# Float32 operands on a 64-byte grid in SBUF: a hybrid decoder step with its dense input halves and gathered expert tokens moved

## The reference

```python
# layer 0: gated DeltaNet mixer, dense SwiGLU; layer 1: short gated convolution, experts
proj = x @ w_in                      # 1024 -> 4112 columns, then conv, silu, delta rule, gate
y = o @ w_out
h = layer_norm(ALPHA * h + y)
h = layer_norm(ALPHA * h + (silu(h @ w_g) * (h @ w_u)) @ w_down)          # d_ff 2816
proj = h @ sc_w_in                   # 1024 -> 3072, gate, 3-tap conv, gate, @ sc_w_out
...
logits = h @ w_router; top_v, top_i = top_k(logits, 2); gates = softmax(top_v)
for e in range(8):                   # d_ff 3584
    y = y + swiglu(h, w_gu[e], w_down[e]) * combine[..., e:e + 1]
h = layer_norm(ALPHA * h + y)
```

## The kernel before

| tile | row pitch, bytes | begins at | rows begin (mod 64) |
|---|---|---|---|
| `raw`, `low` | 8192 | 16512 (0) | 0 |
| `high` | 8192 | 73856 (0) | 0, and 0 for each 128 columns |
| `xres` | 1056 | 108000 (32) | 32, 0, 32, 0, ... |
| `xhb` | 1064 | 116448 (32) | 32, 8, 48, 24, 0, 40, 16, 56 |
| `xlb` | 1064 | 124960 (32) | 32, 8, 48, 24, 0, 40, 16, 56 |
| `xgh`, `xgl` | 512 | 116448 (32), 120544 (32) | 32 |
| `hh`, `hl` | 1056 | 135040 (0), 158272 (0) | 0, 32, 0, 32, ... |
| `yh`, `yl` | 1056 | 163712 (0), 172928 (0) | 0, 32, 0, 32, ... |
| `hth`, `htl` | 2048 | 167808 (0), 171904 (0) | 0 |

## Time and profile before

### The profile page before, as it was taken

The page is one execution under the profiler, slowest core; times in us unless marked ns, Lnnn a source line. Parts: engine busy times, 40 slices in busy tenths (PEclk is TensorE's granted clock), DMA queues, the critical chain, the costliest instruction groups (busy, mean ns, idle before and its releaser), DMA issues.

```text
span 1610.9 us, 23679 instructions
## 1 busy us (share of the span) xinstructions
PE 1564.9 (97%) x8965; PEld 1356.3 (84%) x8965; DVE 1288.0 (80%) x1295; ACT 1052.2 (65%) x963; POOL 103.9 (6%) x155
## 2 busy tenths in 40 slices
PE   8899999999999999999999999999999999999995
PEld 7799989999999997888888888888888888888883
DVE  5786545688546768889889889889889889889897
ACT  5984334676325455777777777778778778777772
POOL 3105000011000011000000000000000000003100
PEclk9999999999999999999999999999999999999998
DMA  9747604598555547999999999999999999999991
GB/s 280 232 134 260 242 2 154 167 289 312 187 164 183 184 132 268 379 372 364 383 369 363 383 370 364 382 370 364 382 369 366 382 368 366 382 368 364 391 397 48
DMA packets 227446, 476.66 MB, mean 296 GB/s; under 512 B 9692, under 2 KB 69100, under 8 KB 227081
## 3 DMA queue, kind: packets, MB, share of 16 engines
q1 hardware_dynamic: 216040, 435.66, 75.6%
q0 software_dynamic: 11344, 40.12, 7.4%
HBM read 449.74 MB, written 26.24 MB: 295 GB/s over the span
## 4 chain that ended last, share of the span: by engine, by line
PE 90%; ACT 5%; DVE 3%; issue 1%; DMA 0%; DVEq 0%; SPq 0%; ACTq 0%
PE bank L2085 13%; PE bank L2082 13%; PE bank L2081 13%; PE bank L2110 13%; PE bank L385 10%; PE bank L2116 6%; PE bank L391 5%; PE bank L1956 2%; PE bank L2093 2%; PE bank L1784 1%; PE bank L1805 1%; PE bank L1961 1%; ACT high L345 1%; PE bank L1802 1%; PE bank L396 1%
## 5 line engine op out<-in xcount | busy, mean ns | idle before, releaser
L350 DVE TENSOR_TENSOR low<-raw,high 128x2048 fp32r<-128x2048 f32 x405 | 923.3, 2290 | 170.5 <-ACT high L345 170.0
L345 ACT ACTIVATE high<-raw 128x2048 fp32r<-128x2048 f32 x405 | 775.1, 1917 | 320.0 <-PE bank L2085 105.3
L2081 PE MATMUL bank<-high,xgh 128*128 128x512 f32 x896 | 359.9, 402 | 0.6 <-DVE xgl L1518 0.6
L2082 PE MATMUL bank<-high,xgl 128*128 128x512 f32 x896 | 356.2, 398 | 0.0
L2085 PE MATMUL bank<-low,xgh 128*128 128x512 f32 x896 | 247.5, 398 | 3.4 <-DVE low L350 3.4
L2085 PEld LDWEIGHTS bank<-low,xgh 128*128 128x128 f32 x896 | 168.8, 189 | 47.5 <-DVE low L350 7.0
L2081 PEld LDWEIGHTS bank<-high,xgh 128*128 128x128 f32 x896 | 169.3, 189 | 39.4 <-issue 1.0
L2082 PEld LDWEIGHTS bank<-high,xgl 128*128 128x128 f32 x896 | 169.3, 189 | 38.9
L385 PE MATMUL bank<-xhb,high 128*128 128x266 f32 (+1 forms) x752 | 158.6, 292 | 3.6 <-ACT tail_nat L874 2.2
L385 PE MATMUL bank<-xlb,high 128*128 128x266 f32 (+1 forms) x752 | 155.4, 288 | 0.0
L2110 PE MATMUL bank<-high,hth 128*128 128x512 f32 x448 | 140.6, 395 | 0.0
(11 more groups left out here) (412 smaller groups left out, 1599.8 us busy)
## 6 DMA issues: line engine op xcount, KB each, us to landing
raw<-in_moe_w_gu_dram SPq DMA_DIRECT2D x224, 1024.0 KB, 5.4
raw<-in_moe_w_down_dram SPq DMA_DIRECT2D x112, 1024.0 KB, 5.2
raw<-in_ffn_w_gu_dram SPq DMA_DIRECT2D x22, 1024.0 KB, 5.4
raw<-in_gdn_w_in_dram SPq DMA_DIRECT2D x16, 1024.0 KB, 11.5
tok<-zeros POOLq DMA_DIRECT2D x26, 512.0 KB, 18.1
raw<-in_sc_w_in_dram SPq DMA_DIRECT2D x12, 1024.0 KB, 5.1
raw<-in_ffn_w_down_dram SPq DMA_DIRECT2D x11, 1024.0 KB, 4.9
s<-in_state_gdn_S_dram POOLq DMA_DIRECT2D x8, 512.0 KB, 7.1
```

Source lines behind the costliest of these rows:

```text
L345: eng.activation(high[:, n % SPLIT, :], raw[:, n % RAW, :], ACT.Copy).then_inc(high_ready, 1)
L350: eng.tensor_tensor(low[:, n % RAW, :], raw[:, n % RAW, :], high[:, n % SPLIT, :].bitcast(F32), ALU.subtract).then_inc(low_ready, 1)
L2081: pe.matmul(out, xgh[:, 4 * kh + k, :], wh[:, k, :], start=kh + k == 0, stop=False)
L2082: pe.matmul(out, xgl[:, 4 * kh + k, :], wh[:, k, :], start=False, stop=False)
```

## The change

The change moves and pads tiles and touches no instruction. `norm_w` and `eps` share one tile (32 bytes less), so that everything behind them begins 32 bytes earlier. The rows of `xhb` and `xlb` get a pitch of 272 float32 (1088 bytes, 17 x 64), while their views keep 266 columns. `region`, where all later tiles start, is rounded up to a multiple of 128, and lies 384 bytes later than before. The order of the instructions is the same on every engine, and so are their shapes.

```diff
+PITCH = -(-WIDE // 16) * 16
...
-        norm_w = place("norm_w", [128, 1])
-        eps = place("eps", [128, 2])
+        scalars = place("scalars", [128, 3])
+        norm_w, eps = scalars[:, 0:1], scalars[:, 1:3]
...
-        xhb = place("xhb", [128, KT, WIDE], F32R)
-        xlb = place("xlb", [128, KT, WIDE], F32R)
+        xhb = place("xhb", [128, KT, PITCH], F32R)[:, :, 0:WIDE]
+        xlb = place("xlb", [128, KT, PITCH], F32R)[:, :, 0:WIDE]
...
         kS = place("kS", [128, HEADS, NS])
+        cursor[0] += -cursor[0] % 128
         region = cursor[0]
...
-        Vn = place("Vn", [128, NCH, HEADS, 128], at=xs_at + 4 * KT * WIDE)
+        Vn = place("Vn", [128, NCH, HEADS, 128], at=xs_at + 4 * KT * PITCH)
```

## The result

The changed kernel takes 1616.26 us (median of 20 runs, 1612.98 to 1622.23) against 1613.22 for the kernel before: a ratio of 1.0021 with an interval of [1.0013, 1.0029]. Forecast were 1591, with a range of 1584 to 1613, and a gain of 1.3%. The kernel became slower by 0.2%. The page of the changed kernel, lines for the earlier trace rows: busy time of PE, its clock in 40 slices, the chain by engine.

The account below looks back on a forecast made before the run. The prediction took PE's matmul pace as the bound. Experts 18.6 us plus dense rows 3.0 made 21.6 us off the profiled execution's 1612.6: 1591 us, with a range of 1584 to 1613.

Parts of the forecast that it names:

- PE's pace is the time of this kernel: Whole kernel: PE is busy 97% of the span, so an address change acts only through the pace of the bounding engine.
- The address, not bank or order, makes 234 out of 227 ns: Experts: gate and up matmuls take 234 ns, down 227, because their stationary operand lies 32 bytes off the grid.
- Rival A: Experts: PSUM bank or order sets the pace, gate and up slots stay at 2.81 us; 1610 to 1613 us, chance 0.21.
- The 64-byte grid is the rule: Experts: tokens on the 64-byte grid bring gate and up slots from 2.81 to 2.72 us, 2.5 us for each expert.
- 18.6 us: Expert stage: total forecast gain, 17.6 us from seven experts and 1.0 from the eighth.
- "Zero" for everything behind `region`: Remaining tiles: xres, Vn, wab, wr come onto the grid, aS and kS leave it; claimed effect zero.
- The eighth expert gains 1.0 us: Last expert: bytes from DMA set its end, so it gains 1.0 us, between nothing and the full 2.5.
- Dense rows gain 3 us: Dense stages: about 2,640 matmuls on xhb or xlb gain 1.3 ns each from the grid; taken as 3 us.
- The settling: Experts: the pace settles once operands permit; a first down slot entered from a slow stretch lasts 2.76 us, not 2.72.
- C: Expert and dense matmuls: rows and weight blocks beginning in equal phase collide, 1 ns each, 5.3 us slower: 1618; chance 0.05.
- B: A 16-byte grid suffices, so experts gain nothing and only half the dense rows gain, 3.4 us: 1609; chance 0.07.
- D: Experts and dense rows: PE reaches the better pace only in parts, half of 18.6 and 3: 1600; chance 0.07.

Follow-up runs that it names:

- e3: Kernel before with only the gathered tokens xgh and xgl moved to 116608, distance 0 modulo 256 from the weights' buffers: 1597.29 us, ratio 0.9904.
- m1: Model left out, PE alone: expert streams of 48 matmuls of 512 columns, stationary block's address swept in steps of 32 bytes; 226.7 ns at distance 0, 233.3 at 64.
- e8: Changed kernel with the expert stage's tiles 128 bytes lower, hth at 168064, distance 0 modulo 256: 1609.92 us, ratio 0.9990.
- e2: Kernel before with only region moved up by 384 bytes; tokens and dense input rows keep their places: 1616.81 us, ratio 1.0026.
- e6: Changed kernel with expert tiles 384 bytes lower and tokens back at 116448, leaving the dense part of the change: 1612.36 us, ratio 0.9996.
- e1: Changed kernel with the expert stage's tiles 384 bytes lower, hth and htl at their old addresses, tokens still moved: 1611.26 us, ratio 0.9991.
- m2: Model left out, PE alone: dense streams of 96 matmuls at old, new and swept places and pitches; pitch 1536 took 11.74 us at distance 0.

## Why the prediction was wrong, point by point

1. **PE's pace is the time of this kernel.** Right. In the expert loop PE is busy 760 of 760 us after as before, and every period in the table is the paces' sum: e3's 336 gate and up matmuls x 6.4 ns and 168 down ones x 1.6 ns are 2.4 us, and 121.2 - 118.9 = 2.3.

2. **The address, not bank or order, makes 234 out of 227 ns.** Right, shown by m1 and e3. Rival A had been given 0.21. Its evidence, two paces of 235 ns of weights against weights, was too short a stretch to bear it: by the starts in the traces their mean is 234 ns before, and with no address of theirs changed it is 231.5 in e3 and 230.5 in e8. The page that the prediction set against the address (the Trainium skill, TensorE: Matmul & The Clock Gate, Step-by-step) says that the weight load does not take from the running matmul's reads. The runs here don't bear that out for float32r: in m1, with no other engine at work, it was 226.7 or 234.2 ns by nothing but the place of the weight block. How the one read delays the other, no run shows.

3. **The 64-byte grid is the rule.** Wrong, and this is the step on which 18.6 us rested. The prediction compared one slow place (32 off the grid) with one fast place (on it) and named the first property that differed. The same two places differ by 96 and 0 modulo 256, and also in their distance to the moving rows. Of the eight residues modulo 256 that m1 tried, 0 is fast, 192 nearly so, and 64 and 128, on the grid like these, are not: 226.7, 228.9, 233.3 and 232.1 ns. The change puts the tokens at 64. The gate and up slot was to fall to 2.72 us and fell to 2.80. The profile of before couldn't decide it, with only two places in it; that should have stood against the 0.60.

4. **"Zero" for everything behind `region`.** Wrong, and it set the sign. The table of places called `hth` and `htl` "384 later, as before", which is true modulo 64 and false modulo 256. A rule with a longer period leaves a shifted operand of 1,344 matmuls an open price. It was 3.5 ns x 1,344 = 4.7 us by the paces (e2's whole time: 1616.81 against 1613.11 us).

5. **The eighth expert gains 1.0 us.** Its mechanism fits the rows, its size was too high: with the tokens on a good place it gained nothing (e3: 82.4 us behind the last `xrow` against 81.8), and ACT waited for loads more often, as forecast. In the changed kernel there was no faster pace that it could have gained from.

6. **Dense rows gain 3 us.** Mis-sized: 264 columns gained 1.1 of the 1.3 ns, but there are 912 of them, and the 1,632 with 266 columns lost 0.4 ns instead. Net 0.4 us, nothing that e6 could measure.

7. **The settling.** Right only in part. The first down slot was long before (2.76 us) with the tokens at 96; in e3, with the tokens at 0, it lasts 2.72 (997.21 to 999.93). But a slow stretch ahead does not do it by itself: in e1 the gate and up slots are slow too (233.4 ns, tokens at 64), and the first down slot lasts 2.73 us. And inside a slow slot nothing settles: m1's streams keep their slow pace over all 48 matmuls.

8. **The rivals.** C named the right side and nearly the right time (1618), which was luck, since its mechanism is wrong: no collision of equal phases; equal phase is the fastest. B, a grid of 16 bytes, falls with m1 too: all of m1's places are multiples of 32. D expected half of a gain that didn't come at all. The rival that was missing is the one that came, a rule with a longer period under which the change moves one operand from a bad place to another bad one and the second from the best place to a bad one.

9. **The clock.** No step spoke of it. It adds some 7 us to 12 of the 28 executions and lifts the median from about 1614.3 to 1616.3. Without it the time would still have lain above the forecast's range and beyond the time before.

10. **Small slips in the sums.** The last `xrow` load of the earlier trace rows is at 1504.3, not 1504.1 us; the period stays 121.2. A full gain of the eighth expert would have added 1.5 us to the 1.0 already counted, not 2.5. Neither changes the forecast.

## What to carry to other kernels

A tile's address is an operand like any other: list for each hot matmul the distance between its stationary and its moving block before and after, and not only for the tiles that the change means to move. With two places in a trace, any rule that tells them apart fits; when the gain rests on such a rule, a stream of 48 matmuls at eight addresses tests it, and here it found 1% (e3: 0.9904) that the grid had missed. A kernel's executions can fall into two groups: look at the clock of each execution before a difference of 3 us is given to one cause.

## What the runs showed of the hardware

- A float32r matmul of 128x512 with its own weight load takes 226.7 ns at full clock where the two operands' addresses are equal modulo 256 bytes, 228.9 where the stationary one is 192 further, 232.1 or 233.3 at 128, 233.3 at 32, 64, 160 and 224, and 234.2 to 234.5 at 96 (m1). With DMA, DVE and ACT at work beside it, it takes 227.6 ns in e3, the entries of the slots included. Matmuls without a weight load of their own were not tried.
- With 264 columns and one distance for all rows it takes 120.0 ns at 0, and 120.0 or 123.3 at 128 (m2, second halves of the streams: L97, L85, L109).
- The Trainium skill (SBUF — State Buffer, Specifications) gives a cacheline of 16 bytes. All places in m1 are multiples of 32, and their paces differ by 3%: the rule seen here is another one, with a period of 256 bytes but for the two paces at 128.
- Around the end of 48 matmuls of 8 columns the granted clock falls to half in all twelve traces of the whole kernel. It came back after 3 to 4 us or after some 27 us in the same program (0.94 and 0.51 over the same 28 us).
